# Transposed residual, time steps from the latent product, wider value products and stored gain rows in a two-part fp32 block kernel

## The chip, the cores and the metric

The kernel runs on one core of one Trainium2 chip. The metric is the device time of one launch in microseconds (us), the median over several runs.

## What is computed

The program runs a first network of two layers on a sequence of 256 tokens with 1024 features, and then a second block. All is in fp32.

- First network, per layer: a mixer (a gated depthwise convolution, a differential attention of four heads and a memory attention), a projection `mixed @ w_out`, then `x = layer_norm(ALPHA * x + mixed, ...)`, then a feed-forward network with a squared ReLU, residual and norm again.
- Second block: `h = rmsnorm(x)` scaled and shifted by a conditioning vector, then `h @ w_in` gives the latents of an attention (256 columns of queries, 128 of keys/values, 64 of index keys, 16 of index weights), a gated state-space part (z, xbc and 32 columns `dt_raw`, one per head) and two gates. The index scores choose the 64 best keys of each query, 16 heads attend over one shared 128-wide key that is also the value, and the result goes through `w_uv` and `w_o_attn`. The state-space part uses `dt = softplus(dt_raw + dt_bias)`. Both parts are gated and added, go through `w_out`, are normed and multiplied by a gain per feature (`post_norm` times a gate of the conditioning vector), and added to x. A gated feed-forward network follows in the same form, with a second gain.

## The kernel before

Engines run programs of their own and meet through semaphores. Weights are streamed by SP (SyncE) through a ring of three 2 MB slots (`ring`); a slot is loaded again when PE (TensorE) has released it. The release is a semaphore increment on a matmul: the helper `mm` (line 1838) attaches it to the next matmul that does not stop an accumulation, if one is owed (`to_release`). Large products (feed-forward, the gates, the output projections) are done as seven products of half size (`seven`, line 1992) in the place of eight, with sums of weights made by DVE (VectorE) and combinations made by ACT (ScalarE) and DVE. Small products go through four PSUM banks `acc` in rotation: PE fills one (`filled`), ACT copies it out (`drained`).

The places that the change touches, in order of time:

- **Residual, both layers.** `with_residual(t)` (2085) writes ALPHA*x plus bias, which lies feature-major in `y`, token-major into two PSUM banks by eight fp32 matmuls against the identity; `token_tile` accumulates `w_out`'s product onto it. It is called in attention slots k = 9 and k = 11 (2209, 2215), between the score, transpose and value products of the attention.
- **Latents.** The first weight unit of the block (464 columns) gives queries, keys/values, index keys and index weights; 80 rows of one bank hold the last two. PE turns keys and index weights to token-major (2356, 2358), ACT copies them (908, 909). Then PE makes index queries and queries while ACT and DVE make the index scores (912, 1474).
- **xbc and attention.** PE makes the 16 banks of xbc (2408). From bank FIRST2 = 7 on, the 16 attention steps are put between them, two to a bank: `scores2` one step ahead, `transposes`, `values2`. `values2` (2400) makes the values of two heads by four matmuls, two per head, each with 128 moving columns. DVE makes `logits2` and `attention` (the division) and the convolution of the bank before.
- **Time steps.** `time_steps(0)` and `time_steps(1)` (2434) are two groups of eight matmuls of `h` with a 1024x32 weight that has a load of its own (486). One group stands ahead of the `w_uv` product and one behind it; then PE waits for all banks (`ready(56)`, 2453) and starts the two units of `w_o_attn`. ACT and DVE make softplus between (955 to 957, 1576 to 1589).
- **Gain rows.** The two gains lie feature-major in `mcol[:, 2:4]` (1435, 1436). DVE spreads them to diagonals (1714), PE multiplies ones by them in four groups `gain_half` (2530) of four matmuls, ACT copies each to `gain_rows` (`row_out`, 1019). The groups stand behind units 4, 6 and 7 of the tail and between the two products of the first token tile of `w_out` (2554, 2579). DVE multiplies by `gain_rows` from 1686 and 1778 on. POOL (GpSimd) makes only sums (`token_sums2`, 564) in the second block.

The order of all this is written out by hand. No planner is involved.

Of the kernel before, what the change touches and what calls it, by code (L numbers as in the profile page):

```python
# [20 lines left out]
P = 128  # L21
# [90 lines left out]
def block_units():  # L112
# [5 lines left out]
    units = [[("w_in_2", 0, 8, 0, COL_Z, 0)], [("w_qidx_2", 0, 2, 0, 1024, 0)], [("w_uq_2", 0, 2, 0, 2048, 0)]]  # L118
# [73 lines left out]
def build(nc, a, out, stop=None):  # L192
    with ExitStack() as ctx:  # L193
# [108 lines left out]
        w_dt = blank[:, 0:DC * SSD_HEADS].rearrange("p (k n) -> p k n", k=DC)  # L302
        strips = nc.dram_tensor("strips", (4 * P * 2 * T + T,), F32).ap()
        strip_rows = nc.dram_tensor("strip_rows", (4, 2 * T), F32).ap()
# [13 lines left out]
        def halves3(t, kn):  # L318
# [31 lines left out]
        gain_diags = [mid[:, 8 + 4 * i:12 + 4 * i, :].rearrange("p a (i n) -> p (a i) n", n=P) for i in range(2)]  # L350
# [54 lines left out]
        diag_ready, ssq_ready, ssum_ready, rdown_ready, ygain_ready = map(sem, (  # L405
            "diag_ready", "ssq_ready", "ssum_ready", "rdown_ready", "ygain_ready"))
# [13 lines left out]
        zsum_ready, ada_scaled, sattn_ready, w_dt_in = sem("zsum_ready"), sem("ada_scaled"), sem("sattn_ready"), sem("w_dt_in")  # L420
        row_full, row_back, xn_low, xn_high, turn_full, h2_low, h2_high = map(sem, (
            "row_full", "row_back", "xn_low", "xn_high", "turn_full", "h2_low", "h2_high"))
# [13 lines left out]
        def _(sp):  # L436
# [45 lines left out]
            for n, parts in enumerate(BLOCK_UNITS):  # L482
                s = n % RING
                slot_free(DEPTH * LAYER_UNITS + n)
                if n == RING:
                    sp.dma_start(w_dt[:, :, :], a["w_in_2"][:, COL_DT:COL_DT + SSD_HEADS].rearrange("(k p) n -> p k n", p=P)).then_inc(w_dt_in, 16)
# [17 lines left out]
        def _(pool):  # L504
# [59 lines left out]
            def token_sums2(base, a11, a12, a21, a22, s1, s2, s3, s4):  # L564
# [7 lines left out]

            pool.wait_ge(cb_full, 1)
# [13 lines left out]
        def _(act):  # L587
# [302 lines left out]
            copied(kvki[0:80, 1, :], b[0:80, 1, :])  # L890
# [18 lines left out]
            copied(widx[:, :, :], b[:, 1, 0:32].rearrange("p (t c) -> p t c", t=TT), scale=16 ** -0.5 * 64 ** -0.5)  # L909
# [45 lines left out]
            act.wait_ge(dt_sum, 1)  # L955
            steps.link(act.activation(dte[:, :, :], dte[:, :, :], ACT.Exp, scale=-1.0))
            act.activation(dte[:, :, :], dte[:, :, :], ACT.Ln, bias=1.0).then_inc(dt_log, 1)
# [61 lines left out]
            def row_out(n):  # L1019

                act.wait_ge(row_full, n + 1)
                act.activation(gain_rows[n // 2][:, n % 2, :], back_high, ACT.Copy, scale=float(D)).then_inc(row_back, 1)

# [24 lines left out]
            row_out(0)  # L1048
            first_bank2(G_SSD)
            inverse_rms2(2, 4.0, 4 * RMS_EPS)  # L1050
            row_out(1)
            first_bank2(G_SSD + 1)
            row_out(2)
# [6 lines left out]
            for t in range(TT):  # L1060
                for h in range(2):
# [7 lines left out]
                    if n == 0:  # L1069
                        row_out(3)  # L1070
# [30 lines left out]
        def _(dve):  # L1101
# [334 lines left out]
            steps.mark(tt(mcol[:, 3, :], mod2[:, 40:48], pcol[:, 2, 88:96], ALU.mult))  # L1436
            steps.sync()
# [13 lines left out]
            for ci in range(6, 8):  # L1451
                bias_steps(ci)

# [102 lines left out]
            def attn_sums(u):  # L1556
# [15 lines left out]
            bank_out(55)  # L1572
# [3 lines left out]
            bank_out(56)  # L1576
            dtb = per_head[:, 0:1, :].broadcast_to([P, TT, SSD_HEADS])
            steps.link(tt(dtv[:, :, :], dtv[:, :, :], dtb, ALU.add))
            stt(dte[:, :, :], dtv[:, :, :], -1.0, dtv[:, :, :], ALU.mult, ALU.max).then_inc(dt_sum, 1)
# [5 lines left out]
            dve.wait_ge(dt_log, 1)  # L1585
            steps.link(stt(dtp[:, :, :], dtv[:, :, :], 0.0, dte[:, :, :], ALU.max, ALU.add))
            dve.wait_ge(dt_exp, 1)
            stt(da[:, :, :], dtp[:, :, :], -1.0, expa[:, :].unsqueeze(1).broadcast_to([P, TT, SSD_HEADS]), ALU.mult, ALU.mult)\
                .then_inc(da_ready, 1)
# [78 lines left out]
            def combine2_tokens(k, h, which):  # L1668
# [17 lines left out]
                dve.wait_ge(row_back, 2 * which + h + 1)  # L1686
# [27 lines left out]
            for i in range(2):  # L1714
                tt(gain_diags[i], ident[:, :].unsqueeze(1).broadcast_to([P, DC, P]), mcol[:, 2 + i, :].unsqueeze(2).broadcast_to([P, DC, P]),
                   ALU.mult).then_inc(diag_ready, 1)
# [55 lines left out]
            for t in range(TT):  # L1772
                for h in range(2):
# [4 lines left out]
                    dve.wait_ge(row_back, h + 1)  # L1778
# [54 lines left out]
        def _(pe):  # L1833
# [4 lines left out]
            def mm(dst, w, m, start, stop):  # L1838

                ins = pe.matmul(dst, w, m, start=start, stop=stop, skip_group_check=True)  # L1840
# [208 lines left out]
            for l in range(DEPTH):  # L2049
# [35 lines left out]
                def with_residual(t):  # L2085

                    for c in range(DC):
                        mm(out_bank[t][c // 4][:, c % 4 * P:(c % 4 + 1) * P], y[:, c, t * P:(t + 1) * P], ident[:, :], c % 4 == 0, False)
# [247 lines left out]
            for k in range(DC):  # L2336
                ins = mm(b[0:80, 1, :], w[:, k, 384:464], y[:, k, :], k == 0, k == DC - 1)
# [19 lines left out]
            for t in range(TT):  # L2357
                ins = mm(b[:, 1, 16 * t:16 * t + 16], kvki[64:80, 1, t * P:(t + 1) * P], ident[64:80, 64:80], True, True)
# [73 lines left out]
            pe.wait_ge(w_dt_in, 16)  # L2432

            def time_steps(t):

                b = free_bank()
                for k in range(DC):
                    ins = mm(b[:, 0, 0:SSD_HEADS], y[:, k, t * P:(t + 1) * P], w_dt[:, k, 0:SSD_HEADS], k == 0, k == DC - 1)
                ins.then_inc(filled, 1)

            time_steps(0)

            w = next_unit().rearrange("p k n -> p (k n)")
            pe.wait_ge(o_drained, DEPTH * STEPS + STEPS2 + 1)
            for j in range(4):
# [4 lines left out]
                ins.then_inc(filled, 1)  # L2450
            time_steps(1)
# [78 lines left out]
            def gain_half(n):  # L2530

                pe.wait_ge(diag_ready, n // 2 + 1)
                pe.wait_ge(row_back, n)
                if n == 1:
                    pe.wait_ge(ms_ln, 2)
                for c in range(4):
# [137 lines left out]
```

## Time and profile before

| | us |
|---|---|
| median of 3 runs (range) | 1387.41 (1387.18 to 1387.93) |
| profiled execution, its own time | 1387.62 |
| its span | 1385.8 |
| PE busy | 1366.5 |
| DVE busy | 907.6 |
| ACT busy | 393.0 |
| POOL busy | 135.4 |

The span is what the profile's rows cover; the remaining 1.8 us of that execution lie around it. An fp32 matmul is two records in the profile (two passes over the moving columns), a transpose is one. Durations of single records overlap their neighbours, so the cost of a group of matmuls is read from where it starts to where the next one starts. PEld rows are the weight loads, which run ahead of the matmuls.

### The profile page before, as it was taken

What the parts mean: (1) busy time and instruction counts of PE and PEld (TensorE: products, weight loads), DVE (VectorE), ACT (ScalarE), POOL (GpSimd) and SP (SyncE); (2) the same over time, 40 slices, a digit from 0 to 9 for tenths busy, and PEclk for the clock granted to TensorE, in tenths of its full rate; (3) what the DMA queues carried; (4) which work ended last, traced back from release to release, by engine and by line L of the source; (5) the groups of instructions that cost most, each with busy time, mean ns of one, the idle gap of its engine ahead of it and who ended that gap; (6) DMA issues with size and microseconds to landing.
All of it is one profiled execution on the core that took longest, in us unless ns stands there. A gap on an engine that the chain in (4) does not pass through costs nothing. (4 is left out here: it accounts for less than half of the span.)

```text
span 1385.8 us, 20855 instructions
## 1 busy us (share of the span) xinstructions
PE 1366.5 (99%) x8729; PEld 1212.2 (87%) x8729; DVE 907.6 (65%) x1512; ACT 393.0 (28%) x821; POOL 135.4 (10%) x112
## 2 busy tenths in 40 slices
PE   8999999999999999999999999999999999999997
PEld 7886899988888599988988889889889995999986
DVE  3765798555387498866642877764668853766653
ACT  2153333220227134321165114443222203101100
POOL 3200322020100034022000000001000100010110
PEclk9999999999999999999999999999999999999999
DMA  9631567666442077567331333053324534455450
GB/s 316 210 122 61 183 249 261 220 243 243 159 146 94 32 262 263 203 241 272 117 126 61 122 122 122 16 183 122 122 72 173 183 137 160 129 183 183 151 183 32
DMA packets 125677, 224.45 MB, mean 162 GB/s; under 512 B 6261, under 2 KB 33165, under 8 KB 125329
## 3 DMA queue, kind: packets, MB, share of 16 engines
q1 hardware_dynamic: 123338, 218.26, 45.7%
q0 software_dynamic: 1840, 4.67, 1.0%
q8 instruction: 70, 1.15, 0.3%
q10 hardware_dynamic: 407, 0.20, 0.1%
q14 instruction: 22, 0.18, 0.0%
HBM read 222.06 MB, written 2.11 MB: 162 GB/s over the span
## 5 line engine op out<-in xcount | busy, mean ns | idle before, releaser
L1840 PE MATMUL acc<-y,ring 128*128 128x256 f32 (+1 forms) x1344 | 247.8, 341 | 0.5 <-DMA ring<-in_w_ffn_in 0.3
L1840 PEld LDWEIGHTS acc<-y,ring 128*128 128x128 f32 x1344 | 214.4, 190 | 24.9 <-issue 2.8
L1840 PE MATMUL acc<-x,ring 128*128 128x128 f32 (+1 forms) x960 | 160.7, 324 | 0.0
L1840 PEld LDWEIGHTS acc<-x,ring 128*128 128x128 f32 x960 | 144.5, 191 | 12.3 <-issue 1.0
L1840 PE MATMUL acc<-ring,big 128*128 128x256 f32 (+1 forms) x376 | 115.5, 453 | 0.0
L1840 PEld LDWEIGHTS acc<-ring,big 128*128 128x128 f32 x376 | 70.6, 190 | 33.3 <-issue 26.5
L1840 PE MATMUL acc<-ring,hid 128*128 128x256 f32 (+1 forms) x364 | 99.0, 417 | 0.5 <-DVE hid L1735 0.5
L1840 PEld LDWEIGHTS acc<-ring,hid 128*128 128x128 f32 x364 | 68.3, 190 | 21.9 <-issue 14.5
L810 ACT ACTIVATE ring<-ring,silc 128x512 f32<-128x512 f32 x96 | 60.1, 709 | 95.3 <-DMA ring<-in_ada_w 95.3
L1167 DVE TENSOR_TENSOR ring<-ring 128x2048 f32<-128x2048 f32 (+1 forms) x24 | 42.3, 1763 | 36.5 <-ACT ring L810 36.1
L1840 PE MATMUL acc<-ysq,ring 128*128 128x128 f32 x528 | 64.1, 275 | 0.3 <-ACT dtv L845 0.3
L1840 PEld LDWEIGHTS acc<-ysq,ring 128*128 128x128 f32 x528 | 61.4, 192 | 0.4 <-ACT dtv L845 0.4
L1840 PE MATMUL scr<-ysq,ring 128*128 128x128 f32 x496 | 60.5, 275 | 0.0
L1840 PEld LDWEIGHTS scr<-ysq,ring 128*128 128x128 f32 x496 | 57.9, 192 | 0.0
L1343 DVE SCALAR_TENSOR_TENSOR mid<-upad,pc,mid 128x256 f32<-128x256 f32 x120 | 47.9, 485 | 0.0
L658 ACT ACTIVATE work<-work,nm 128x256 f32<-128x256 f32 x80 | 39.7, 497 | 26.0 <-DVE nm L1516 16.5
L1227 DVE TENSOR_TENSOR ring<-ring 128x1024 f32<-128x1024 f32 x32 | 45.4, 1419 | 0.0
L1226 DVE TENSOR_TENSOR mid<-ring 128x1024 f32<-128x1024 f32 x16 | 19.5, 1222 | 35.5 <-DMA ring<-in_w_down 22.4
L1468 DVE SCALAR_TENSOR_TENSOR big<-pre,pcol,big 128x256 f32<-128x256 f32 x96 | 40.0, 479 | 0.0
L1840 PE MATMUL acc<-big,ring 128*128 128x256 f32 x160 | 37.3, 385 | 1.4 <-DMA ring<-in_w_mem_kv 1.4
L1000 ACT ACTIVATE big<-acc 128x512 f32<-128x512 f32 x19 | 11.3, 596 | 94.3 <-PE acc L1840 94.3
L1840 PEld LDWEIGHTS acc<-big,ring 128*128 128x128 f32 x160 | 29.6, 190 | 8.8 <-issue 2.9
(477 smaller groups left out, 2486.4 us busy)
## 6 DMA issues: line engine op xcount, KB each, us to landing
ring<-in_w_in SPq DMA_DIRECT2D x24, 2048.0 KB, 8.8
ring<-in_w_up SPq DMA_DIRECT2D x16, 2048.0 KB, 8.8
ring<-in_w_down SPq DMA_DIRECT2D x16, 2048.0 KB, 8.0
ring<-in_ada_w SPq DMA_DIRECT2D x12, 2048.0 KB, 13.7
ring<-in_w_ffn_in SPq DMA_DIRECT2D x22, 1024.0 KB, 7.2
ring<-in_w_out SPq DMA_DIRECT2D x6, 2048.0 KB, 8.0
ring<-in_w_o_ssd SPq DMA_DIRECT2D x4, 2048.0 KB, 8.6
ring<-in_w_ffn_out SPq DMA_DIRECT2D x4, 2048.0 KB, 7.7
```

The lines of the kernel that those rows point to most:

```text
L658: ins = act.activation(pr[:, i % 2, j, :], lg[:, i % 2, j, :], ACT.Exp, bias=nm[:, i % 2, j:j + 1], accum_out=zz[:, i % 2, j:j + 1])
L810: act.activation(ring[:, n % RING, k, :], ring[:, n % RING, k, :], ACT.Copy, scale=silc[:, 1, k:k + 1]).then_inc(ada_scaled, 1)
L1000: act.activation(quads[:, 6:8, :], acc[2 * ((k + 1) % 2)][:, :, :], ACT.Copy).then_inc(ma_free, 1)
L1167: steps.link(tt(w[:, 0:width, :], w[:, 0:width, :], w[:, width:2 * width, :], ALU.add))
L1226: tt(t[:, 0], b12, b11, ALU.subtract).then_inc(t_ready, 1)
L1227: tt(b12, b22, b12, ALU.subtract).then_inc(t_ready, 1)
L1343: ins = stt(cy[:, c, :], upad[:, c, tap:tap + T], w, cy[:, c, :], ALU.mult, ALU.add)
L1468: ins = stt(xbc[:, c, :], src, w, xbc[:, c, :], ALU.mult, ALU.add)
L1840: ins = pe.matmul(dst, w, m, start=start, stop=stop, skip_group_check=True)
```

## The change

- The eight matmuls of `with_residual` get `is_transpose=True`.
- The 32 columns of `dt_raw` are loaded behind the 464 of the first unit, by a second DMA of that unit; the bank's product has 112 rows in the place of 80, and the turn to token-major is 48 columns wide in the place of 16. ACT copies `dtv` there. `time_steps` and its separate load go. The softplus chain moves: on DVE ahead of the index scores, on ACT between the copies of index queries and queries. The bank rotation is kept in step by counting two banks more behind the `w_uv` product.
- `values2` makes both heads by two matmuls with 256 moving columns.
- `scores2(0)` is issued in the middle of the bank FIRST2 - 1 and no longer at the start of bank FIRST2.
- `gain_half`, `row_out` and the diagonals go. POOL writes the 16 columns of `mcol[:, 2:4]` to a DRAM tensor, one DMA for each, once DVE has made them; behind its second `token_sums2` and the last product that reads the buffer, it loads both rows back with a broadcast to 128 partitions. DVE waits for these loads.

```diff
-    units = [[("w_in_2", 0, 8, 0, COL_Z, 0)], ...
+    units = [[("w_in_2", 0, 8, 0, COL_Z, 0), ("w_in_2", 0, 8, COL_DT, SSD_HEADS, COL_Z)], ...
...
+        gain_store = nc.dram_tensor("gain_store", (2, D), F32).ap()
...
-                if n == RING:
-                    sp.dma_start(w_dt[:, :, :], a["w_in_2"][:, COL_DT:COL_DT + SSD_HEADS]...).then_inc(w_dt_in, 16)
...  POOL
+            pool.wait_ge(gains_ready, 1)
+            for w in range(2):
+                for c in range(DC):
+                    pool.dma_start(gain_store[w:w + 1, c * P:(c + 1) * P].rearrange("o p -> p o"), mcol[:, 2 + w, c:c + 1]).then_inc(gains_out, 16)
             pool.wait_ge(cb_full, 1)
             token_sums2(32, ...)
             pool.wait_ge(gy_ready, 8)
             token_sums2(36, ...)
+            pool.wait_ge(gains_out, 16 * 2 * DC)
+            pool.wait_ge(mc_full, TAIL_G + G_Z + 4)
+            for w in range(2):
+                pool.dma_start(gain_rows[w], gain_store[w:w + 1, :].rearrange("o (h d) -> o h d", h=2).broadcast_to([P, 2, 512])).then_inc(gains_in, 16)
...  ACT
-            copied(kvki[0:80, 1, :], b[0:80, 1, :])
+            copied(kvki[0:112, 1, :], b[0:112, 1, :])
...
-            copied(widx[:, :, :], b[:, 1, 0:32].rearrange("p (t c) -> p t c", t=TT), scale=16 ** -0.5 * 64 ** -0.5)
+            token_cols = b[:, 1, 0:96].rearrange("p (t c) -> p t c", t=TT)
+            act.activation(dtv[:, :, :], token_cols[:, :, 16:48], ACT.Copy)
+            copied(widx[:, :, :], token_cols[:, :, 0:16], scale=16 ** -0.5 * 64 ** -0.5)
...
             for j in range(4):
                 copied(qi2[:, 2 * j:2 * j + 2, :], full()[:, :, :])
+            act.wait_ge(dt_sum, 1)
+            steps.link(act.activation(dte[:, :, :], dte[:, :, :], ACT.Exp, scale=-1.0))
+            act.activation(dte[:, :, :], dte[:, :, :], ACT.Ln, bias=1.0).then_inc(dt_log, 1)
...
-            copied(dtv[:, 0, :], full()[:, 0, 0:SSD_HEADS])
             for j in range(4):
-                copied(ysq[:, 2 * j:2 * j + 2, :], full()[:, :, :], scale=0.5)
-            copied(dtv[:, 1, :], full()[:, 0, 0:SSD_HEADS])
-            (wait for dt_sum, Exp, Ln)
+                act.activation(ysq[:, 2 * j:2 * j + 2, :], full()[:, :, :], ACT.Copy, scale=0.5).then_inc(drained, 3 if j == 3 else 1)
+            bank[0] += 2
...
-                    if n == 0:
-                        row_out(3)
...  DVE
             for ci in range(6, 8):
                 bias_steps(ci)
+            bank_out(21)
+            (the softplus chain: add, max(-x, x), wait dt_log, max and add, wait dt_exp, multiply)
...
-            for i in range(2):
-                tt(gain_diags[i], ident..., mcol[:, 2 + i, :]..., ALU.mult).then_inc(diag_ready, 1)
...
-                    dve.wait_ge(row_back, h + 1)
+                    dve.wait_ge(gains_in, 16 * 2)
...  PE
-                        mm(out_bank[t][c // 4][...], y[:, c, t * P:(t + 1) * P], ident[:, :], c % 4 == 0, False)
+                        mm(out_bank[t][c // 4][...], y[:, c, t * P:(t + 1) * P], ident[:, :], c % 4 == 0, False,
+                           turned=True)
...
-                ins = mm(b[0:80, 1, :], w[:, k, 384:464], y[:, k, :], k == 0, k == DC - 1)
+                ins = mm(b[0:112, 1, :], w[:, k, 384:496], y[:, k, :], k == 0, k == DC - 1)
...
-                for m in range(2):
-                    for kt in range(TT):
-                        ins = pe.matmul(pvb[:, m, :], kvtok[:, kt, :], pt[:, i % 2, 2 * m + kt, :], start=kt == 0, stop=kt == 1)
+                for kt in range(TT):
+                    ins = pe.matmul(pvb[:, 0:2, :], kvtok[:, kt, :], pt[:, i % 2, kt:kt + 3:2, :], start=kt == 0, stop=kt == 1)
...
                 for i in range(2):
+                    if b2 == FIRST2 - 1 and i:
+                        scores2(0)
                     if b2 >= FIRST2:
                         n = 2 * (b2 - FIRST2) + i
-                        if n == 0:
-                            scores2(0)
...
-            time_steps(0)
             w = next_unit().rearrange("p k n -> p (k n)")
             pe.wait_ge(o_drained, DEPTH * STEPS + STEPS2 + 1)
             for j in range(4):
                 (four matmuls, each with start and stop)
-                ins.then_inc(filled, 1)
-            time_steps(1)
+                ins.then_inc(filled, 3 if j == 3 else 1)
+            bank[0] += 2
             to_release[0] += 1
             ready(56)
...
-                    if m != 5:
-                        gain_half((0, None, 1, 2)[m - 4])
...
             mixed_tokens(0, 0)
-            gain_half(3)
             mixed_tokens(0, 1)
```

## Rows read from the trace of the kernel before

**Rows 1.** The page, busy time by engine.
```profile
PE 1366.5 (99%) x8729; PEld 1212.2 (87%) x8729; DVE 907.6 (65%) x1512; ACT 393.0 (28%) x821; POOL 135.4 (10%) x112
```
**Rows 2.** The waits of PE over the whole span: total, times, longest.
```profile
PE ptb L1945 <- DVE work L1157: 1.8, 3, 1.3
...
PE acc L1840 <- DVE hid L1735: 0.5, 1, 0.5
```
**Rows 3.** Instructions by line and form, PE: count, busy us, mean ns.
```profile
L1840 PE MATMUL acc<-ident,y 128*128 128x128 f32 x64 | 7.8, 275 | 0.0
...
L1840 PE MATMUL ptb<-mid,ones 128*128 128x128 f32 x32 | 4.2, 275 | 0.0
```
**Rows 4.** Timeline of layer one, attention slots 9 and 10: start, length, instructions.
```profile
109.62 1.95 PE L1840 MATMUL acc<-ident,y 128*128 128x128 f32 x16
...
110.45 0.62 DVE L1157 TENSOR_SCALAR work<-work,rz 128x256 f32<-128x256 f32 x2
...
111.40 1.03 PE L1936 MATMUL scr<-mid 128*128 128x256 f32 x4
```
**Rows 5.** Timeline, sixteen fp32 transposes in a row and what follows them.
```profile
715.81 1.01 PEld L2318 LDWEIGHTS scr<-ident,x 128*128 128x128 f32 x8
...
717.66 1.17 PEld L1840 LDWEIGHTS acc<-big,ones 128*128 128x128 f32 x6
```
**Rows 6.** Timeline from the first time-step group to the first unit of w_o_attn.
```profile
917.17 1.87 PE L1840 MATMUL acc<-upad,y 128*128 128x32 f32 x16
...
917.50 0.37 SPq L495 DMA_DIRECT2D ring<-in_w_o_attn  x1
...
918.97 3.67 PE L1840 MATMUL acc<-mid,ring 128*64 128x256 f32 x32
...
922.69 0.60 ACT L845 ACTIVATE ysq<-acc 128x512 f32<-128x512 f32 x1 [0.27 <-PE acc L1840]
...
924.83 3.65 PEld L1840 LDWEIGHTS acc<-ysq,ring 128*128 128x128 f32 x32 [0.40 <-ACT dtv L845]
```
**Rows 7.** DMA issues: count, KB each, us from issue to landing.
```profile
ring<-in_w_o_attn SPq DMA_DIRECT2D x2, 2048.0 KB, 7.8
...
hid<-in_ln_g POOLq DMA_DIRECT2D x2, 512.0 KB, 6.7
...
post<-in_positions POOLq DMA_DIRECT2D x2, 0.5 KB, 5.2
```
**Rows 8.** Timeline of the index stage, ACT and DVE around the first query bank.
```profile
748.07 0.60 ACT L845 ACTIVATE mid<-acc 128x512 f32<-128x512 f32 x1 [1.13 <-PE acc L1840]
...
749.78 0.35 DVE L1484 TENSOR_SCALAR big<-work,widx 128x256 f32<-128x256 f32 x1 [20.30 <-ACT work L919]
```
**Rows 9.** Timeline of one attention step of the block, PE.
```profile
841.11 1.03 PE L2397 MATMUL scr<-kvn,mid 128*128 128x256 f32 x4
841.97 0.60 PE L1945 MATMUL ptb<-ident,work 128*128 128x128 f32 x4
842.41 1.06 PE L2405 MATMUL pvw<-pt,kvtok 128*128 128x128 f32 x8
843.30 2.97 PE L1840 MATMUL acc<-y,ring 128*128 128x256 f32 x13
```
**Rows 10.** Timeline of the tail around the gain groups.
```profile
1126.32 0.97 PEld L1840 LDWEIGHTS ptb<-mid,ones 128*128 128x128 f32 x8
...
1127.22 1.87 PEld L1840 LDWEIGHTS acc<-hid,ring 128*128 128x128 f32 x16
...
1140.55 0.69 DVE L1735 TENSOR_TENSOR hid<-big,mid 128x512 f32<-128x512 f32 x1
...
1141.39 7.11 PE L1840 MATMUL acc<-ring,hid 128*128 128x512 f32 x16 [0.50 <-DVE hid L1735]
```
**Rows 11.** Timeline, the first attention step of the block.
```profile
825.19 0.62 DVE L1157 TENSOR_SCALAR work<-work,rz 128x256 f32<-128x256 f32 x2
...
825.86 0.66 PE L1945 MATMUL ptb<-ident,work 128*128 128x128 f32 x4 [1.26 <-DVE work L1157]
```

More of the change, by code:

```diff
@@ L349, in build @@
         gain_rows = [mix_row, gain_row]
-        gain_diags = [mid[:, 8 + 4 * i:12 + 4 * i, :].rearrange("p a (i n) -> p (a i) n", n=P) for i in range(2)]
         ymix = ysq[:, :, :].rearrange("p a b -> p (a b)").rearrange("p (t h d) -> p t h d", t=TT, h=2)
@@ L404, in build @@
         c_step, relu_done = sem("c_step"), sem("relu_done")
-        diag_ready, ssq_ready, ssum_ready, rdown_ready, ygain_ready = map(sem, (
-            "diag_ready", "ssq_ready", "ssum_ready", "rdown_ready", "ygain_ready"))
+        gains_ready, gains_out, gains_in = map(sem, ("gains_ready", "gains_out", "gains_in"))
+        ssq_ready, ssum_ready, rdown_ready, ygain_ready = map(sem, (
+            "ssq_ready", "ssum_ready", "rdown_ready", "ygain_ready"))
         gate_done, mix_step, ms_full, ms_ln = map(sem, ("gate_done", "mix_step", "ms_full", "ms_ln"))
@@ L1435, in _ @@
             steps.mark(tt(mcol[:, 2, :], mod2[:, 16:24], pcol[:, 2, 72:80], ALU.mult))
-            steps.mark(tt(mcol[:, 3, :], mod2[:, 40:48], pcol[:, 2, 88:96], ALU.mult))
-            steps.sync()
+            steps.link(tt(mcol[:, 3, :], mod2[:, 40:48], pcol[:, 2, 88:96], ALU.mult))
+            dve.sem_inc(gains_ready, 1)
             times_rstd(y, x, 1)
@@ L1452, in _ @@
                 bias_steps(ci)
+            bank_out(21)
+            dtb = per_head[:, 0:1, :].broadcast_to([P, TT, SSD_HEADS])
+            steps.link(tt(dtv[:, :, :], dtv[:, :, :], dtb, ALU.add))
+            stt(dte[:, :, :], dtv[:, :, :], -1.0, dtv[:, :, :], ALU.mult, ALU.max).then_inc(dt_sum, 1)
+            dve.wait_ge(dt_log, 1)
+            steps.link(stt(dtp[:, :, :], dtv[:, :, :], 0.0, dte[:, :, :], ALU.max, ALU.add))
+            dve.wait_ge(dt_exp, 1)
+            stt(da[:, :, :], dtp[:, :, :], -1.0, expa[:, :].unsqueeze(1).broadcast_to([P, TT, SSD_HEADS]), ALU.mult, ALU.mult)\
+                .then_inc(da_ready, 1)
             def conv2(b2, taps=range(TAPS2)):
@@ L1570, in _ @@
             conv2(15)
-            bank_out(55)
+            bank_out(56)
             a11, a12, a21, a22 = ysq[:, 0:4, 0:H], ysq[:, 4:8, 0:H], ysq[:, 0:4, H:T], ysq[:, 4:8, H:T]
@@ L1575, in _ @@
             tt(sattn[:, 2], a11, a21, ALU.subtract).then_inc(sattn_ready, 1)
[L1576 to L1579, printed above, removed]
             dve.wait_ge(sattn_ready, 1)
@@ L1584, in _ @@
             attn_sums(1)
[L1585 to L1589, printed above, removed]
             for u in range(2):
@@ L1685, in combine2_tokens @@
                 dve.wait_ge(mz_free, before + 2)
-                dve.wait_ge(row_back, 2 * which + h + 1)
+                dve.wait_ge(gains_in, 16 * 2)
                 for t in range(TT):
@@ L1836, in _, with mm @@
             to_release = [0]
-            def mm(dst, w, m, start, stop):
-                ins = pe.matmul(dst, w, m, start=start, stop=stop, skip_group_check=True)
+            def mm(dst, w, m, start, stop, turned=False):
+                ins = pe.matmul(dst, w, m, start=start, stop=stop, is_transpose=turned, skip_group_check=True)
                 if to_release[0] and not stop:
@@ L2357, in _ @@
             for t in range(TT):
-                ins = mm(b[:, 1, 16 * t:16 * t + 16], kvki[64:80, 1, t * P:(t + 1) * P], ident[64:80, 64:80], True, True)
+                ins = mm(b[:, 1, 48 * t:48 * t + 48], kvki[64:112, 1, t * P:(t + 1) * P], ident[64:112, 64:112], True, True)
             ins.then_inc(filled, 1)
@@ L2430, in _ @@
                     to_release[0] += 1
[L2432 to L2438, printed above, removed]
-                ins.then_inc(filled, 1)
-            time_steps(0)
             w = next_unit().rearrange("p k n -> p (k n)")
@@ L2528, in tail_unit @@
                 to_release[0] += 1
[L2530 to L2536, printed above, removed]
-                    ins = mm(back_high[:, c * P:(c + 1) * P], ones[:, 0, :], gain_diags[n // 2][:, 4 * (n % 2) + c, :], c == 0, c == 3)
-                ins.then_inc(row_full, 1)
             pe.wait_ge(cb_free, SSD_GROUPS)
@@ L2583, in _ @@
             to_release[0] += 1
-            pe.wait_ge(row_back, 4)
+            pe.wait_ge(ms_ln, 2)
             turned(0)
```

26 lines of the change are left out of this document (6 added, 20 removed).

## The prediction

> **What bounds the kernel now.** I read the shares of busy time first, then the waits of PE, then the timeline at each place that the diff touches. PE is busy for 1366.5 of the 1385.8 us of the span [rows 1]; no other engine comes near. The waits of PE are few: 1.8 us in three waits of an attention transpose on DVE's division, 0.5 us before the first `w_out` product on DVE [rows 2]. So a microsecond taken from PE's stream is a microsecond of the end, unless the work taken was the cover of something PE would wait for. The question for each part is therefore how much PE time goes, read as the distance between the start of a group and the start of what follows it, and what PE meets when it comes early.
>
> **Residual by transposes.** There are 64 records of the identity products [rows 3], that is 32 matmuls in four calls of eight. One call stands from 109.62 to 111.40, 1.78 us [rows 4]. Sixteen real transposes take from 715.81 to 717.66, 1.85 us, so eight take 0.925 us [rows 5]: one pass each in the place of two. Saved: 1.78 - 0.925 = 0.86 us a call, 3.4 us for four. Does PE then wait? After the first call come the scores of step 11 (from 111.40, now 110.54) and some 0.87 us later the transposes of step 9, at 111.4; DVE's division for them ends at 110.45 + 0.62 = 111.07 [rows 4]. That is 0.3 us of slack, so I count the whole. The trace has no transpose whose bank is then accumulated on by ordinary matmuls; the bounds are no gain at all (two passes stay) and 3.4 us. I take 3.4, since the nearest rows are transposes with the same operands. The Trainium skill (TensorE: Matmul & The Clock Gate, Terms) says that the transpose mode is four times faster for fp32; here the rows show 1.78 to 0.925, less than twice. By that rule the call would fall to 0.45 us, the four calls would save 5.3 us, and the sum below would be 1.9 us larger.
>
> **Time steps.** The first group stands from 917.17 to 918.97, 1.80 us, and goes whole: what follows needs ACT's copies of the attention outputs, which are done before it. The second group and the wait behind it end at 924.83. Without it PE waits for ACT's copy of the fourth `w_uv` bank, which ends at 922.69 + 0.60 = 923.29, and starts some 0.05 us later, at 923.34: 1.49 us saved and not 1.9, since 1.1 us of the group was cover for that copy [rows 6]. Together 3.3 us. What is added: 112 rows for 80 and 48 columns for 16 in products that cost by their moving columns or by their loads; I take nothing, at most 0.1 us. The softplus chain moves beside the index stage: ACT sits idle for 1.13 us before its first query copy at 748.07, and its two small operations need about 0.6 us (0.26 each by their kind, with one wait between); DVE sits idle for 20.3 us before its first index score [rows 8]. If that cover were gone, PE would be late by the 0.6 us at most. The column load moves to a unit that is fetched tens of us ahead of use.
>
> One thing moves that the diff does not name. The release of the ring slot of the last xbc weights rides on the next matmul that does not stop an accumulation. That was the first matmul of the first time-step group: the load of the second `w_o_attn` unit went out at 917.50 [rows 6]. The `w_uv` matmuls all start and stop at once, so the release now waits for the first unit of `w_o_attn`, at about 923.34 - 1.8 = 921.5 on the new clock. The load takes 7.8 us [rows 7] and lands at about 929.6; PE needs it after seven half products of 1.79 us, at 921.5 + 12.5 = 934.0. It is hidden with 4.4 us to spare.
>
> **Value products.** A step now has four matmuls from 842.41 to 843.30, 0.89 us. Two matmuls with 256 moving columns, the score products, stand from 841.11 to 841.97, 0.86 us [rows 9]. So a step saves 0.03 us and sixteen save 0.5 us: the moving columns are the same, only two loads fall away, and these were hidden. Bounds: nothing, and 1.3 us if the lone groups of 128 columns cost as much more at their ends as the records' busy time suggests (1.06 us against 1.03 and a gap). I take 0.5.
>
> **Gain rows.** There are four groups of four matmuls (32 records, [rows 3]); one stands from 1126.32 to 1127.22, 0.90 us [rows 10]. Three of them give that back: 2.7 us. The one behind the last tail unit does not. Right after it PE waited 0.50 us for DVE, which ends its `mix2` half at 1140.55 + 0.69 = 1141.24; PE starts at 1141.39 [rows 10]. DVE's chain there starts from the last product of that unit and knows nothing of the gain group, so its 0.9 us turns into a wait of 1.4 us. DVE is also freed of two diagonals, ACT of four copies; neither bounds anything. POOL gets 16 small stores and two broadcast loads. Its queue has little else; small pieces landed in 5.2 us and a 512 KB broadcast in 6.7 us before [rows 7]. The loads go out behind POOL's second sums, near 1087, and the first use is near 1149 on the old clock: hidden by some 50 us. If the cover were gone, the loads would cost their whole 7 us. They share the DMA engines with one 2 MB weight unit, which is wanted 10 us and more after it lands.
>
> **First scores ahead.** PE waits 1.26 us for the division of the first step, which ends at 825.19 + 0.62 = 825.81 [rows 11]. Putting `scores2(0)` half a bank (3.45 us) earlier lets DVE make the first logits before the convolution of bank 6. Then DVE's order is convolution half, second logits, division, and it ends at about 824.5; PE, not having waited, comes at 825.86 - 1.26 = 824.6. The whole 1.26 us goes, with 0.1 us to spare. Bounds: 0.6 us, if ACT's copy of bank 6, now 0.86 us later for the scores before it, costs DVE its start, and 1.26. I take 1.2.
>
> **Sum.** 3.4 + 3.3 + 0.5 + 2.7 + 1.2 = 11.1 us. The profiled execution took 1387.62, 0.2 more than the median of 1387.41; taken from the median, 1376.3 us.
>
> **Rivals.**
> 1. *More is absorbed.* PE comes early in four attention slots with 0.3 us of slack at the closest, and in the block's first step with 0.1. If half of the residual's gain and of the first-step wait turns into waits on DVE, the sum loses 1.7 + 0.6 us: 1378.6. For it: that transpose already waited on DVE in three steps [rows 2]. Against: the next steps have over 1 us of slack. Chance 0.18.
> 2. *The residual does not become cheaper* (the flag keeps two passes when the bank is accumulated on). 3.4 us less: 1379.7. Against it are the single records of all transposes. Chance 0.05.
> 3. *More is given back:* the last gain group too (0.9), and the value products at their upper bound (0.8 more): 1374.6. For the first speaks only that DVE has 2.4 us less to do before. Chance 0.12.
> 4. *The transposes fall to a quarter.* As a mechanism of this kernel: eight in 0.45 us where the rows show 0.925. 1.9 us more: 1374.4. This is the rule of the Trainium skill (TensorE: Matmul & The Clock Gate, Terms) named above. By that rule; the trace disagrees in 16 transposes [rows 5]. Chance 0.02.
> 5. *The late ring slot (slower).* Place: PE's wait for the second `w_o_attn` unit. Its load now goes out together with that of the next gate unit, as both slots come free within two matmuls, so it may share bandwidth. If the two 2 MB loads land together, after twice 7.8 = 15.6 us, at 937.1, PE waits 3.1 us: 1379.4. The kernel is slower than before only when the load takes over 12.5 + 11.1 + 2.8 = 26.4 us. For a wait speaks that the release does move by 4 us; against slower, that no such load took half of that. Chance 0.06 for a wait of this kind, 0.01 for slower.
>
> **How the numbers follow.** The forecast has a chance of 0.56, with 1375.3 to 1377.3 about it; the rivals have 0.18, 0.05, 0.12, 0.02 and 0.07. The range reaches down to rivals 3 and 4 and up to rivals 1 and 2's near side: 1374.2 to 1379.2. About 0.2% (2.8 us) is what a measurement of this kernel can tell from no change. All cases but the far end of rival 5 are faster by more than that, and some unforeseen wait would have to take 8 us of 11 for no change: faster 0.97, same 0.02, slower 0.01.
>
> **What would show it.** PE's busy time should fall by about 11 us, and no group of `upad` or of ones with `mid` should be left. Residual: 32 single records of the identity on `y` and about 0.93 us a call. Time steps: the first `w_o_attn` product 0.05 us behind ACT's fourth copy; the load of the second unit issued at that moment, and no wait of PE on it. Values: 64 records, 0.86 us a step. Gain rows: the wait before the first `w_out` product at 1.4 us in the place of 0.5. First scores: the 1.26 us wait gone. I would be wrong if a wait of PE on DVE in the attention slots, or on a DMA at the second `w_o_attn` unit, stands in the list of waits with more than a microsecond, or if the residual's records are still two to a matmul.

## The result and the profile after

| | before | changed |
|---|---|---|
| median, us (range) | 1387.33 (1387.18 to 1387.93) | 1375.88 (1375.65 to 1376.14) |
| runs | 4 | 4 |
| span of the profiled execution | 1385.8 | 1373.9 |
| PE busy | 1366.5 | 1355.1 |

The changed kernel takes 0.9917 of the time before (95% interval 0.99 to 0.9934): 11.45 us less, where 11.1 were forecast. The two profiled spans differ by 11.9 us.

The page of the changed kernel, busy time by engine, to be read against [rows 1]:

```profile
PE 1355.1 (99%) x8569; PEld 1201.1 (87%) x8569; DVE 906.9 (66%) x1510; ACT 389.6 (28%) x816; POOL 147.9 (11%) x130
```

PE has 160 records fewer and 11.4 us less busy time. POOL has 18 instructions more, the 16 stores and two loads. The waits of PE over the whole span of the changed kernel (total, times, longest), to be read against [rows 2]:

```profile
PE acc L1833 <- DVE hid L1728: 1.4, 1, 1.4
PE acc L1833 <- DMA ring<-in_w_mem_kv: 1.2, 1, 1.2
...
PE acc L1833 <- ACT ysq L961: 0.8, 1, 0.8
...
PE ptb L1938 <- DVE work L1152: 0.5, 2, 0.3
```

The transposes' wait for DVE's division has fallen from 1.8 us in three waits to 0.5 in two. The wait that went is that of the block's first step, 1.26 us [rows 11]; the other two were 0.5 us together before and still are: no attention slot took back what the residual gave, and none gave anything. Two rows are waits that the forecast allows for: the `w_out` product waits 1.4 us for DVE in the place of 0.5, and the first `w_o_attn` product waits 0.8 us for ACT's last copy. No wait for a load of `w_o_attn` is in the list.

**Residual.** The line of the identity products by form (count, busy us, mean ns, idle), against [rows 3]: one record for each matmul now, 32 in all.

```profile
L1833 PE MATMUL acc<-ident,y 128*128 128x128 f32 x32 | 4.1, 273 | 0.0
```

The timeline of layer one, slot 9, against [rows 4]: from 109.77 to 110.64 is 0.87 us where 1.78 stood. The scores and the transposes follow without a wait.

```profile
109.77 1.04 PE L1833 MATMUL acc<-ident,y 128*128 128x128 f32 x8
110.64 1.03 PE L1929 MATMUL scr<-mid 128*128 128x256 f32 x4
111.50 0.60 PE L1938 MATMUL ptb<-ident,work 128*128 128x128 f32 x4
```

**First scores and value products.** The timeline of the block's first two attention steps, against [rows 11] and [rows 9]: the transposes at 820.91 have no wait, and a step's values take from 826.16 to 827.02, 0.86 us.

```profile
820.91 0.66 PE L1938 MATMUL ptb<-ident,work 128*128 128x128 f32 x4
821.40 3.62 PE L1833 MATMUL acc<-y,ring 128*128 128x256 f32 x16
...
826.16 1.03 PE L2398 MATMUL pvw<-pt,kvtok 128*128 128x256 f32 x4
827.02 1.68 PE L1833 MATMUL acc<-y,ring 128*128 128x256 f32 x7
```

**Time steps.** The timeline of PE from the `w_uv` product on, against [rows 6]: 4.43 us from its start to `w_o_attn`, where 7.66 stood from the first time-step group on (917.17 to 924.83).

```profile
911.83 3.67 PE L1833 MATMUL acc<-mid,ring 128*64 128x256 f32 x32
916.26 2.50 PE L1833 MATMUL acc<-ysq,ring 128*128 128x128 f32 x20 [0.76 <-ACT ysq L961]
```

The second load of `w_o_attn` went out at 916.78, right behind that product's first matmuls, and landed 8.0 us later; DVE, the first to use it, started at 924.77:

```profile
924.77 1.23 DVE L1567 TENSOR_TENSOR hid<-ring 128x1024 f32<-128x1024 f32 x1 [5.91 <-DMA ring<-in_w_o_attn]
```

**Gain rows.** The tail's timeline, against [rows 10]. The loads by POOL go out at 1078.76 and 1079.32, some 60 us ahead of their first use. Unit 7's last group stands at 1127.69, and the first `w_out` product now waits 1.39 us:

```profile
1078.76 0.57 POOL L583 DMA_DIRECT2D pt<-gain_store  x1
1079.32 0.54 POOL L583 DMA_DIRECT2D work<-gain_store  x1
...
1127.69 1.95 PE L1833 MATMUL pvw<-hid,big 128*128 128x128 f32 x16
1131.04 20.84 PE L1833 MATMUL acc<-ring,hid 128*128 128x512 f32 x48 [1.39 <-DVE hid L1728]
```

One thing was not forecast. The kernel before waits in the second `w_out` tile's stretch for a load of `w_ffn_in`, and the changed kernel does not. In the kernel before the 64 matmuls ahead of the last turn take from 1170.70 to 1178.44, 7.74 us:

```profile
1174.76 3.84 PE L1840 MATMUL acc<-y,ring 128*128 128x128 f32 x32 [0.33 <-DMA ring<-in_w_ffn_in]
1178.44 0.60 PE L2573 MATMUL scr<-ident,hid 128*128 128x128 f32 x4
```

In the changed kernel they take 7.15 us:

```profile
1159.45 7.31 PE L1833 MATMUL acc<-y,ring 128*128 128x128 f32 x64
1166.60 0.60 PE L2542 MATMUL scr<-ident,hid 128*128 128x128 f32 x4
```

### The profile page after: what moved, and what is told of

It is laid out like the page before. It is cut to its first block and busy times, and to the rows that moved or that the text cites. A ratio compares the mean times of both kernels' runs of the same rounds, so it can differ in the third digit from the quotient of the medians.

```text
span 1373.9 us, 20542 instructions
## 1 busy us (share of the span) xinstructions
PE 1355.1 (99%) x8569; PEld 1201.1 (87%) x8569; DVE 906.9 (66%) x1510; ACT 389.6 (28%) x816; POOL 147.9 (11%) x130
## 5 line engine op out<-in xcount | busy, mean ns | idle before, releaser
L1005 ACT ACTIVATE big<-acc 128x512 f32<-128x512 f32 x19 | 11.3, 596 | 114.2 <-PE acc L1833 114.2
L555 POOL TENSOR_TENSOR big<-hid 128x512 f32<-128x512 f32 x8 | 14.4, 1803 | 218.1 <-PE pvw L1833 152.9
```

The lines of the kernel that those rows point to most:

```text
L555: pool.tensor_tensor(s1, a21, a22, ALU.add).then_inc(sh_ready, 1)
L1005: act.activation(quads[:, 6:8, :], acc[2 * ((k + 1) % 2)][:, :, :], ACT.Copy).then_inc(ma_free, 1)
```

## The experiments

The main theory is that every part is PE time and that the parts add. The rivals are those of the prediction. Each kernel below is the changed one with one edit (the last but one has two), and the time before was measured beside it (1387.05 to 1387.16 us). "Cost" is 11.45 us less the distance to that. The kernel before had 1387.33 us where the 11.45 comes from, so each cost carries some 0.2 to 0.3 us that all of them share: against the changed kernel's own 1375.88 us every cost is 0.17 to 0.28 us smaller. The distances inside the traces, collected further below, do not have this error.

**Each part undone by itself.**

Residual:

```diff
-                        mm(out_bank[t][c // 4][...], y[:, c, t * P:(t + 1) * P], ident[:, :], c % 4 == 0, False,
-                           turned=True)
+                        mm(out_bank[t][c // 4][...], y[:, c, t * P:(t + 1) * P], ident[:, :], c % 4 == 0, False)
```

> The changed kernel with its residual as ordinary fp32 matmuls against the identity again; all else as changed. Theory (the residual is PE time in full, eight at a time in four attention calls): the stretch from the first residual matmul to the last is 1.78 us a call where the changed kernel has 0.87, so 4 x 0.91 = 3.6 us more than the changed kernel, 1379.5. Rival, absorbed in the attention slots: half of it is lost in waits for the transposed scores, which are 0.8 us in all in the changed kernel's two attention layers where the kernel before had 3.1: the cost is then some 1.8, 1377.7. Rival, transposes at a quarter of the time: ruled out if the changed kernel's 0.87 us stands; 5.3 us would be wanted.

Measured 1379.51 us (before 1387.16): a cost of 3.8. In its trace the first call takes 1.79 us again:

```profile
109.73 1.95 PE L1833 MATMUL acc<-ident,y 128*128 128x128 f32 x16
111.52 0.81 PE L1929 MATMUL scr<-mid 128*128 128x256 f32 x3
```

That is the full 4 x 0.91 and, by this measure, a little more. The expectation's waits of 3.1 and 0.8 us are not those of PE: its rows have 0.5 us in the two attention layers in both kernels. Absorption by half, which would have left a cost of 1.8, falls; so do the two passes for accumulated banks, and the quarter.

Value products:

```diff
-                for kt in range(TT):
-                    ins = pe.matmul(pvb[:, 0:2, :], kvtok[:, kt, :], pt[:, i % 2, kt:kt + 3:2, :], start=kt == 0, stop=kt == 1)
+                for m in range(2):
+                    for kt in range(TT):
+                        ins = pe.matmul(pvb[:, m, :], kvtok[:, kt, :], pt[:, i % 2, 2 * m + kt, :], start=kt == 0, stop=kt == 1)
```

> The changed kernel with four value products of one head each in a step of the block's attention, not two of both heads. Theory: 32 steps at 0.016 us each, 0.5 us more than the changed kernel, 1376.4. Rival (the fixed part of a matmul is of the size that the gap between two small products suggests, some 0.02 us each of 64): up to 1.3 us, 1377.2. No difference, if DVE sets the pace of these steps.

Measured 1376.06 us: a cost of 0.35, which is at the limit of what medians of four or five runs, with ranges of 0.5, can tell. The step is 0.89 us again (826.02 to 826.91 in its trace), 0.03 more, and the distance over all sixteen steps, given below, is 0.49 us longer. The upper bound of 1.3 falls. The figure of 32 steps in the expectation should read 16 steps at 0.03 us; the 0.5 is the same.

First scores:

```diff
-                    if b2 == FIRST2 - 1 and i:
-                        scores2(0)
                     if b2 >= FIRST2:
                         n = 2 * (b2 - FIRST2) + i
+                        if n == 0:
+                            scores2(0)
```

> The changed kernel with the scores of block attention step 0 issued after, and not ahead of, the last bank's products. Theory: PE waits again at the first transposes for DVE's softmax, 1.26 us in the trace of before; 1.2 to 1.4 us more than the changed kernel, 1377.2, and the wait row 'PE tpp <- DVE' is back with 1.2 to 1.4 us. Rival: the following attention steps run into a wait of their own that took the saved time, so the cost is under 0.5 us.

Measured 1377.08 us: a cost of 1.37. Its timeline has the wait back, and none after it that the changed kernel would be spared:

```profile
819.80 1.03 PE L2391 MATMUL scr<-kvn,mid 128*128 128x256 f32 x4
822.08 0.66 PE L1938 MATMUL ptb<-ident,work 128*128 128x128 f32 x4 [1.26 <-DVE work L1152]
```

From scores to transposes 2.28 us here and 0.87 in the changed kernel (820.04 to 820.91): 1.41. The row's own 1.26 is less than the hole, since the end of the group before is modelled some 0.16 us later than the next could start.

Time steps:

```diff
-            bank_out(21)
-            (the softplus chain on DVE; Exp and Ln on ACT)
...
+            time_steps(0)
             w = next_unit().rearrange("p k n -> p (k n)")
...
+            time_steps(1)
```

> The changed kernel with the block's time steps from the block's input again, by their own load of weights and sixteen products of 32 columns, and no longer from the latent. Theory: between the last product of the block's up-projection and the first of w_o_attn PE is occupied 3.1 to 3.3 us longer; 1379.0. The load of the weights comes back ahead of the second load of w_o_attn, which stays covered. Rival: part of it (the 1.2 us that PE now waits for ACT's fourth copy) was hidden before, so the cost is only some 2, 1378.

Measured 1378.69 us: a cost of 2.98. In its trace the stretch is that of the kernel before (911.34 to 919.00, 7.66 us), 3.23 more than in the changed kernel. So the theory holds and the rival (2 us) falls. Of the 3.23 the changed kernel pays back 0.13. Its last half bank of xbc is followed by the `w_uv` product after 3.55 us (908.28 to 911.83), and here by the first time-step group after 3.45 (907.89 to 911.34); why, the rows do not show. Another 0.03 lies between the turn to token-major and the attention.

Gain rows (the code of before, with PE, ACT and DVE, in the place of POOL's DMAs):

```diff
-            pool.wait_ge(gains_ready, 1)
-            (16 stores, later 2 loads)
...
+                    if m != 5:
+                        gain_half((0, None, 1, 2)[m - 4])
...
+            gain_half(3)
```

> The changed kernel with the four gain half-rows made on PE (sixteen products of ones with a diagonal), DVE and ACT again, no DRAM in between. Theory: 3 x 0.9 = 2.7 us for three groups, the fourth, ahead of the tail unit whose opening product waits for DVE's LayerNorm sums, for nothing; and some 0.55 more, because the second fp32 wait at the load of w_ffn_in (0.33 to 0.52 us, gone in the changed kernel) may belong to the later arrival of the tail: 2.7 to 3.3 us, 1378.5 to 1379.1. Rival: all four count, 3.6 us, 1379.4. Rival: that wait has nothing to do with the gain rows, 2.7 sharp.

Measured 1378.39 us (before 1387.05): a cost of 2.8. The first `w_out` product waits 0.50 us again, not 1.39: three groups count, the one after unit 7 does not, and the 3.6 of the rival falls. The wait for `w_ffn_in` is back in part. Its 64 matmuls take 7.43 us, 0.28 more than in the changed kernel, and this is part of the cost.

**Is the place after unit 7 free?** One group of four unused fp32 products, ones by the identity, is added at two places. It writes half a bank that nobody reads.

```diff
+                    if m == 7:      # the second kernel: m == 6
+                        pe.wait_ge(ms_ln, 2)
+                        for i in range(4):
+                            mm(back_high[:, i * P:(i + 1) * P], ones[:, 0, :], ident[:, :], i == 0, i == 3)
```

> The changed kernel with one added group of four unused products (ones by the identity) after tail unit seven, the place whose next product waits 1.39 us for DVE. Theory: 0.9 us of work fits in that wait, cost 0.0 to 0.2, 1375.9. Rival: the wait was only renamed in the trace and PE is the bound there: 0.9, 1376.6.

> The same four unused products one unit earlier, after tail unit six. Theory: no wait of PE stands behind it until the LayerNorm, whose sums come only after unit seven's product, so 0.9 us in full, 1376.6 to 1376.7. Rival: what is added ahead of the tail's wait is swallowed by it as well: 0, as in the place after unit seven.

Measured 1375.52 us after unit 7 (a cost of -0.1) and 1376.38 after unit 6 (0.8), both beside 1387.05. The same 0.9 us of PE work costs nothing in one place and nearly all of itself one unit (seven groups of 1.79 us) earlier. The timeline of the kernel with the group after unit 7:

```profile
1127.39 1.95 PE L1833 MATMUL pvw<-hid,big 128*128 128x128 f32 x16
1129.17 1.06 PE L1833 MATMUL ptb<-ident,ones 128*128 128x128 f32 x8
1130.73 2.81 PE L1833 MATMUL acc<-ring,hid 128*128 128x512 f32 x6 [0.50 <-DVE hid L1728]
```

From 1127.39 to 1130.73 is 3.34 us, and it is 3.35 in the changed kernel. DVE's chain sets this distance. That is why the fourth gain group gave nothing back. The 0.1 us that this kernel seems to gain stands ahead of the edit: in the profiled executions it comes to unit 7's last group 0.30 us earlier than the changed kernel (1127.39 and 1127.69), and has been as much earlier since the first residual product (109.47 and 109.77). Counted from there to the first `w_out` product the two added groups cost -0.01 and 0.88 us.

**How near is the late ring slot?** The release of both owed slots, and so the second load of `w_o_attn` and the next gate load, is held back by four half products.

```diff
+            held = to_release[0]
+            to_release[0] = 0
...
+                if u == 0:
+                    seven(w, attn_t[u], ..., opening[0:4], True, True)
+                    to_release[0] = held
-                      ..., usual if u else opening, True, True)
+                      ..., usual if u else opening[4:], True, True)
```

> The changed kernel with the release of both ring slots (and so the load of the second w_o_attn unit) held back until four of w_o_attn's half products are done, some 7.1 us. Theory: the load's landing has 4.0 us to spare before PE needs it, so PE now waits some 3 us at it (a row 'PE <- DMA ring<-in_w_o_attn' or '<- DVE' behind it) and the kernel takes 3 us more, 1378.7. Rival: the slot has far more to spare than 4.0 us since DVE's copy is not needed by PE: no difference. Rival: the delayed loads now collide with the next ones and cost over 5 us.

Measured 1380.08 us (before 1387.11): a cost of 4.4, not 3. Counted from the first `w_o_attn` product, the issue went from 0.52 us behind it (916.26 to 916.78) to 7.66 us behind it (915.93 to 923.59), 7.1 us later, and the row of PE's wait has 2.69:

```profile
926.75 1.95 PE L1833 MATMUL acc<-mid,ring 128*128 128x128 f32 x16
931.39 3.04 PE L1833 MATMUL acc<-ysq,ring 128*128 128x128 f32 x16 [2.69 <-DMA ring<-in_w_o_attn]
934.23 2.63 PE L1833 MATMUL acc<-mid,ring 128*128 128x128 f32 x16
```

The hole itself is 2.85 us: the group from 926.75 takes 1.79, and the next starts at 931.39. So the slack in the changed kernel is 7.1 - 2.85 = 4.3 us, of which 0.2 is the load's faster landing here (7.8 us for 8.0). This fits the 4.0 read from the changed kernel's trace (landed at 924.8, wanted at 928.8); 4.4 were forecast. The wait's size was right, its price was not. The groups behind it take 2.84 and 2.46 us in the place of 1.79, 1.7 us more together. The busy times by stretch in the same execution show where they lose it (columns: stretch and its length, then busy us with the count for PE, PEld, DVE, ACT and POOL, the granted clock, DMA share, GB/s):

```profile
925.00:928.70 3.70, 3.70 (x34) 3.50 (x32) 0.00 (x0) 0.00 (x0) 0.00 (x0) 1.00 0.94 362
928.70:931.40 2.70, 0.01 (x1) 0.01 (x1) 0.03 (x1) 0.60 (x1) 0.00 (x0) 1.00 1.06 391
931.40:934.40 3.00, 3.00 (x17) 3.00 (x18) 3.00 (x3) 0.00 (x0) 0.00 (x0) 0.64 0.99 360
934.40:937.00 2.60, 2.60 (x20) 2.60 (x19) 2.53 (x5) 0.00 (x0) 0.00 (x0) 0.76 1.04 396
937.00:940.00 3.00, 3.00 (x29) 3.00 (x28) 1.59 (x4) 0.60 (x1) 0.00 (x0) 1.00 1.05 390
```

The price is not the same in each execution. Four of the five took 1379.97 to 1380.21 us; the fifth took 1378.65, with a mean granted clock of 0.999 where the others had 0.997 and 0.998. That is a cost of 3.0 us, the forecast price. There is no trace of that execution, so it is only likely, and not shown, that its clock stayed at 1.00 behind the wait.

**Can the two new waits be filled?** The first kernel starts `w_out`'s first product when half of its operand is there, the second starts `w_o_attn`'s first half product ahead of the wait for ACT's last copy, the third does both. None changes what is computed.

```diff
+            pe.wait_ge(mix2_ready, 1)
+            mixed_tokens(0, 0, range(0, DC // 2))
             pe.wait_ge(mix2_ready, 3)
-            mixed_tokens(0, 0)
+            mixed_tokens(0, 0, range(DC // 2, DC))
```

> The changed kernel with the first product of w_out on tokens begun when the first half of the normalised residual is ready (its chunks 0 to 3), the rest of it behind the wait for the second half. Theory: PE waits there for the whole of it, 1.4 us in the trace; the four half products take 4 x 0.22 = 0.9 us, and they move into that wait: 0.9 to 1.4 us less, 1374.5 to 1375.0. Rival: DVE's chain behind sets the end, nothing is gained.

```diff
-            ready(56)
+            ready(52)
...
+                if u == 0:
+                    seven(w, attn_t[u], ..., opening[0:1], True, True)
+                    ready(56)
-                      ..., usual if u else opening, True, True)
+                      ..., usual if u else opening[1:], True, True)
```

> The changed kernel with w_o_attn's first half product begun when the first weights are in, and the wait for ACT's last copy of the block's up-projection moved behind it. Theory: PE's wait there, 0.76 us at the product and 1.21 us at its weight load, is filled with a half product of 1.8 us: 0.8 to 1.2 us less, 1374.7 to 1375.0. Rival: the first half product needs that copy's bank drained later anyway and only the wait moves: no difference.

> Both of the reorderings that take a wait of PE away: w_out's first product on tokens begun at the first half of the normalised residual (1.75 us less than the changed kernel when done alone), and w_o_attn's first half product ahead of the wait for ACT's last copy (0.8 to 1.2 less by its theory). Additive: 1372.8 to 1373.1. Rival: the tail's start moved by the one takes cover from a wait behind it (the load of w_ffn_in, whose second wait went when the tail came 11 us earlier), up to 0.6 us given back.

Measured 1373.85 us (before 1387.05), 1.75 less than the changed kernel; 1374.72 (before 1387.11), 0.94 less; and 1373.11, 2.55 less. The first kernel gained more than its range, for three reasons. The hole is larger than the row that names it: 1127.69 to 1131.04 holds 1.79 us of products and so 1.56 of hole. The four products that fill it have 512 moving columns and take 0.87 us each (eight of them stand from 1141.39 to 1148.33 in the kernel before), not 0.22, so they fill it whole. And the rest is scatter: by the distance inside the traces the gain is 1.57 us, and that of the second kernel 0.83, the 4.43 us of its stretch less the 3.60 of the `w_uv` product. The kernel with both edits has neither wait:

```profile
1126.69 1.95 PE L1833 MATMUL pvw<-hid,big 128*128 128x128 f32 x16
1128.47 7.03 PE L1833 MATMUL acc<-ring,hid 128*128 128x512 f32 x16
```

Both together give 0.14 us less than their sum of 2.69, within the scatter; by the distances they give 2.39 where 1.57 and 0.83 make 2.40. At 1373.11 us, 0.99 of the time before (0.9885 to 0.9915), it is the fastest of all.

**The wait for `w_ffn_in`.** The kernel before was profiled a second time, without an edit.

> The kernel before, profiled a second time. Open is the wait for the load of w_ffn_in in the tail (0.33 us of PE, the load landing 9.4 us after its issue), which the changed kernel does not have (7.8 us). If it belongs to the kernel before, the landing is again 9.1 to 9.4 us and PE's row for the 64 products shows 0.3 to 0.6 us more than the changed kernel's 7.15 from start to next start. If it is chance of one execution, the landing is near 7.8 and the wait is absent.

That execution took 1387.32 us with a span of 1385.5. Of the two loads issued at 1164.8 the longer landed 9.2 us after its issue; the 64 matmuls take 7.53 us, 0.38 more than in the changed kernel. The longer landing and those 64 matmuls, kernel by kernel:

| kernel | landing, us | the 64 matmuls, us |
|---|---|---|
| before, twice | 9.4, 9.2 | 7.74, 7.53 |
| gain rows undone | 9.1 | 7.43 |
| residual undone | 8.9 | 7.24 |
| changed | 7.8 | 7.15 |

The other kernels whose landing was read had 7.6 to 8.8 us, and none of them has the wait (their 64 matmuls take 7.14 or 7.15 us). So the wait is not the chance of one execution. Three executions, in two kernels, landed after 9.1 us or more, and both kernels make their gain rows on PE. Why a load lands later there stays open; its issue stands at the same distance from PE's products in both.

## Why the prediction was right

| part | forecast | by the traces | by undoing it |
|---|---|---|---|
| residual | 3.4 | 4 x 0.91 = 3.6 | 3.8 |
| time steps | 3.3 | 7.66 - 4.43 = 3.2 | 3.0 |
| value products | 0.5 | 16 x 0.03 = 0.5 | 0.35 |
| gain rows | 2.7 | 3 x 0.9 = 2.7 | 2.8 |
| first scores | 1.2 | 1.4 | 1.4 |
| wait for `w_ffn_in` | - | 0.6 | not by itself |
| sum | 11.1 | 12.0 | 11.3 |

The five undone parts sum to 11.3 of the 11.45 us, but to 10.3 where each is counted from the changed kernel's own median, so the medians alone do not settle whether the parts add. The traces do. All kernels are alike up to the first residual product, and the executions come to it at 109.41 to 109.77 us, the changed kernel last of all. The distance from there to the first `w_out` product of the block has none of this scatter:

| kernel | first residual product | first `w_out` product | distance | more than changed |
|---|---|---|---|---|
| changed | 109.77 | 1131.04 | 1021.27 | |
| residual undone | 109.73 | 1134.64 | 1024.91 | 3.64 |
| time steps undone | 109.41 | 1133.78 | 1024.37 | 3.10 |
| value products undone | 109.62 | 1131.38 | 1021.76 | 0.49 |
| gain rows undone | 109.48 | 1132.61 | 1023.13 | 1.86 |
| first scores undone | 109.53 | 1132.21 | 1022.68 | 1.41 |
| before | 109.62 | 1141.39 | 1031.77 | 10.50 |
| before, again | 109.54 | 1141.31 | 1031.77 | 10.50 |

The mark lies behind two of the three gain groups that count. The five sum to 10.50, the whole distance: the parts are independent, and PE's stream is the whole path. Behind this mark lie the gain group between the first two `w_out` products (1148.33 to 1149.22, 0.89 us) and the wait for `w_ffn_in` (0.59). Together that is 12.0 us, against 11.9 between the spans of the two profiled executions, of which the changed kernel's later start took 0.15. The medians differ by 0.4 us less than the spans. So that 11.1 came within 0.35 us of 11.45 is in part luck: against 12.0 the sum was 0.9 us short, in the residual, the first scores and the unforeseen wait, while what the time steps paid back (0.13) lay the other way.

- *Residual.* The step was right, with a size of 0.87 us a call for 0.925. The 0.925 was read from rows of weight loads [rows 5]; by the rows of PE the same sixteen transposes of before take 1.75 us, 0.87 for eight:

```profile
716.02 1.04 PE L2318 MATMUL scr<-ident,x 128*128 128x128 f32 x8
...
717.77 2.09 PE L1840 MATMUL acc<-big,ones 128*128 128x256 f32 x8
```

  The flag gives one record for each matmul also where ordinary matmuls accumulate on the bank afterwards, which no row of before showed. A record of 128 moving columns takes 0.11 us either way (1.78 us over 16, 0.87 over 8): what halves the time is their number. What the prediction calls a pass is such a record. The slack of 0.3 us in the attention slots was enough; the waits there stayed at 0.5 us. The Trainium skill (TensorE: Matmul & The Clock Gate, Terms) gives four times for fp32; the 0.87 us against 1.78 say 2.05, and the row decides.
- *Time steps.* Right in both halves: the first group went whole, the second up to ACT's fourth copy. The copy ended at 916.21, and PE started at 916.26, 0.05 us behind it as forecast. The "1.1 us of cover" in the prediction, which its sum does not use, was too much: the second group started at 922.57, so its cover was 923.34 - 922.57 = 0.77 us, and the hole that is left is 0.83. The 0.13 us that the changed kernel pays elsewhere is near the bound of 0.1.

```profile
922.57 1.97 PE L1840 MATMUL acc<-upad,y 128*128 128x32 f32 x16
```

  The load was later, as it had to be with its release on a `w_o_attn` matmul, and had 4.0 us of slack.
- *Gain rows.* Right that one of the four groups is not a gain (the 2.8 by undoing holds 0.3 us of the wait for `w_ffn_in`), and the two added groups showed where a group costs and where not. The loads from DRAM landed in 5.6 and 8.0 us under 60 us of cover.
- *First scores.* The term was 0.2 us too small: the wait's row was taken for the hole. The division now ends at 820.86 and PE comes at 820.91, so the slack is 0.05 us and the gain is used up.
- *Rivals.* More absorbed, unchanged residual, more given back and the late slot all fell. The two loads that go out together did not share their time as rival 5 feared: that of `w_o_attn` landed after 8.0 us and the gate unit's after 12.9. For a wait there the prediction's price was incomplete: one of some 3 us cost 4.4 in four of five executions, and 3.0 in one.

What was missed is the wait for `w_ffn_in` (0.59 and 0.38 us in the two profiles of before). The prediction did not list it among the terms, as no step of the change touches that load.

## What to carry to other kernels

Here, with one engine busy for 99% of the span, the parts of the change added, and each could be priced as the distance from the start of a group to the start of the next; what has to be found is the place where another engine's chain, and not the busy one, sets that distance, as after tail unit 7. Removed work that stood in front of such a chain leaves a hole, and the hole can be filled by splitting the next product so that it starts on the half of its operand that is ready: that was worth 2.4 us more here. Tell a hole by these distances, since an idle row can be 0.16 us smaller. And where the medians of two kernels scatter by as much as the part in question, count in their traces from one mark to another that both have: what happens ahead of the first mark then drops out, which told 0.49 us here where the medians gave 0.2 or 0.35.

## What the hardware did that was not expected

- A wait whose row has 2.69 us cost 4.4 by the median of five executions. The granted clock was 1.00 up to the wait and in it, and the clock was 0.64 in the first 3.0 us behind it and 0.76 in the next 2.6, a mixture of the levels 1.2 and 2.4 GHz, before it was 1.00 again. The wait of 1.39 us in the tail of the changed kernel had 1.00 in every stretch around it. The Trainium skill (TensorE: Matmul & The Clock Gate, Part 1) says that the clock follows how busy PE has been; this run agrees in kind. One of its five executions was 1.4 us shorter, so the same edit does not cost it each time.
- The longer of two 1 MB loads, issued at the same distance from PE's products in every kernel, landed after 7.6 to 9.4 us, with a margin for PE of about 8.8; the kernel before got 9.4 and 9.2 in its two profiles, for a reason that these runs do not show.
